# A hybrid decoder layer on one core: the depth of the key loads, the place of the residual loads, and the order of VectorE's small steps

## The reference

```python
h = rms(x, g_pre); z = h @ w_in                     # w_in: 1024 x 3584
ua, va, ga, qb, kb, vb, gb = split(z)               # 512 columns each
ya = gelu(ua) * (tril(w_s) @ rms_group(gelu(va)) + b_s)
yb = attend(qb, kb, vb)                             # prompt: causal; sample: see below
y  = concat(rms(ya) * silu(ga), rms(yb) * silu(gb)) @ w_out
out = x + rms(y, g_post)
```

## Time and profile before

| | us |
|---|---|
| median of three runs | 464.26 |
| lowest and highest of them | 460.81, 469.82 |
| the profiled execution's own time | 458.46 |
| its span, first to last instruction | 456.7 |
| mean granted TensorE clock in it | 0.952 of full speed |

### The profile page before, as it was taken

The page is one execution under the profiler, slowest core; times in us unless marked ns, Lnnn a source line. Parts: engine busy times, 40 slices in busy tenths (PEclk is TensorE's granted clock), DMA queues, the critical chain, the costliest instruction groups (busy, mean ns, idle before and its releaser), DMA issues.

```text
span 456.7 us, 8866 instructions
## 1 busy us (share of the span) xinstructions
PE 404.6 (89%) x2696; PEld 189.1 (41%) x2696; DVE 278.5 (61%) x756; ACT 125.2 (27%) x282; POOL 243.6 (53%) x347
## 2 busy tenths in 40 slices
PE   4898998999599997999998979999699289979993
PEld 2643443434243453445534434444244144434361
DVE  2445494458244596678767875678675975782242
ACT  2411110000121323664656332642461321001110
POOL 4877226661666236751877456734575467672021
PEclk9899998999899999999999997999799689997998
DMA  7999269984999629993999489937999899642121
GB/s 226 408 380 364 77 204 376 343 232 150 315 361 296 192 76 321 346 257 103 292 338 282 123 278 354 280 90 225 346 358 289 238 365 343 175 98 52 46 93 49
DMA packets 79694, 111.24 MB, mean 244 GB/s; under 512 B 46560, under 2 KB 47584, under 8 KB 79648
## 3 DMA queue, kind: packets, MB, share of 16 engines
q0 software_dynamic: 22576, 71.45, 46.0%
q1 hardware_dynamic: 44864, 21.10, 17.7%
q10 hardware_dynamic: 12208, 18.14, 13.4%
HBM read 106.34 MB, written 4.29 MB: 242 GB/s over the span
## 4 chain that ended last, share of the span: by engine, by line
PE 43%; DMA 19%; issue 11%; DVE 10%; POOL 7%; SPq 6%; DVEq 2%; POOLq 1%; ACT 0%; ACTq 0%
PE PA L1027 24%; DMA K<-in_cache_k,kidx 12%; POOL K L890 6%; PE PA L1133 5%; DVE ksum L1609 4%; PE GB L1150 4%; PE SB L981 3%; SPq L774 3%; DMA V<-in_cache_v 2%; DMA V<-in_page_table 2%; PE SB L1081 2%; PE DC L1179 1%; DMA q_rows<-qs 1%; DVEq L1607 1%; PE PO L1103 1%
## 5 line engine op out<-in xcount | busy, mean ns | idle before, releaser
L890 POOL DMA_INDIRECT K<-in_cache_k,kidx x128 | 134.5, 1051 | 128.0 <-DVE ksum L1609 67.8
L1027 PE MATMUL PA<-wbuf,hT 128*128 128x512 f32 x384 | 188.5, 624 | 1.8 <-DMA wbuf<-in_w_in 0.9
L741 DVE TENSOR_TENSOR ksum<-K 128x512 f32<-128x512 f32 x128 | 85.9, 687 | 59.5 <-DMA K<-in_cache_k,kidx 33.8
L1027 PEld LDWEIGHTS PA<-wbuf,hT 128*128 128x128 f32 x384 | 69.1, 196 | 79.6 <-issue 74.9
L726 POOL DMA_DIRECT2D V<-in_cache_v x128 | 76.0, 593 | 32.6 <-issue 24.6
L1133 PE MATMUL PA<-wbuf,hT 128*128 128x512 f32 x128 | 62.1, 627 | 3.1 <-DVE v L1539 2.2
L1609 DVE TENSOR_TENSOR ksum<-K,qb 128x128 f32<-128x128 f32 x192 | 41.9, 286 | 12.6 <-DVE selT L1579 4.8
L1133 PEld LDWEIGHTS PA<-wbuf,hT 128*128 128x128 f32 x128 | 23.9, 199 | 30.4 <-issue 29.9
L1150 PE MATMUL GB<-ksum,win 128*32 128x512 f32 x256 | 34.1, 605 | 1.3 <-DVE ksum L741 1.3
L1027 PE MATMUL PA<-hT,wbuf 128*128 128x512 f32 x64 | 31.0, 630 | 0.0
L1624 DVE TENSOR_REDUCE sc<-ksum 128x48 f32<-128x3072 f32 x8 | 26.8, 3353 | 0.3
(11 more groups left out here) (200 smaller groups left out, 371.1 us busy)
## 6 DMA issues: line engine op xcount, KB each, us to landing
wbuf<-in_w_in ACTq DMA_DIRECT2D x20, 512.0 KB
V<-in_cache_v SPq DMA_DIRECT2D x240, 32.0 KB
V<-in_cache_v POOLq DMA_DIRECT2D x128, 32.0 KB, 3.0
wbuf<-in_w_out ACTq DMA_DIRECT2D x8, 512.0 KB
wbuf<-in_w_in SPq DMA_DIRECT2D x8, 256.0 KB, 8.6
K<-in_cache_k,kidx POOLq DMA_INDIRECT x128, 7.7
wbuf<-in_w_in SPq DMA_DIRECT2D x4, 512.0 KB
qb<-q_rows SPq DMA_DIRECT2D x8, 256.0 KB
```

The source lines that it names most:

```text
L741: eng.tensor_tensor(ksum[:, n % SUMS, :], K[:, n, 0, :], K[:, n, 1, :], ALU.add).then_inc(s_dsum, 1)
L890: pool.indirect_dma_start(K[:, n, :, :].rearrange("p r w -> p (r w)"), None, k_rows, bass.IndirectOffsetOnAxis(ap=kidx[:, b, n:n + 1], axis=0)
L1027: last = pe.matmul(bank[:, :], lhs, rhs, start=(kc == 0), stop=(kc == KC - 1))
```

## The change

The number of key blocks on their way is four. The order of lanes on VectorE is "score norm scale out gate attention groups sample tail". The four pairs of small loads, gpostq and xq, are issued by SyncE among the first loads, after the last of the small weights. The step res becomes five steps, g_post first and then the four residual tiles; they follow the squares of yb in the plan, where before they needed only the last values of the attention. VectorE waits for g_post before the first op, for the residual tiles before the first opf, and for the small loads before the sample's last step. vn has four slots, and the gb chunk uses all four: its tiles 2 and 3 wait for nothing, its tiles 0 and 1 for the ga products of tiles 2 and 3.

```diff
-                if t >= 2 or name == "gb":
-                    deps.append(("DVE", ("pj", c, t - 2) if t >= 2 else ("pj", c - 1, t + 2)))
+                if (name == "ga") == (t >= 2):
+                    deps.append(("DVE", ("pj", 5, t - 2 if name == "ga" else t + 2)))
...
-        add("DVE", "out", ("op", t, half), 0.8, ("ACT", ("op", t, half)), ("ACT", ("res",)))
+        add("DVE", "out", ("op", t, half), 0.8, ("ACT", ("op", t, half)), ("ACT", ("res", 0)))
...
-            add("DVE", "scale", ("opf", t), 1.3, ("POOL", ("op", t, 1)))
+            add("DVE", "scale", ("opf", t), 1.3, ("POOL", ("op", t, 1)), ("ACT", ("res", NT)))
...
-    add("ACT", "fetch", ("res",), 2.5, ("PE", ("pv", H - 2, NT - 1)), ("SP", ("vrow", NT)))
+    for r in range(NT + 1):
+        add("ACT", "fetch", ("res", r), 0.55, ("ACT", ("sq", 1, NT - 1)), ("SP", ("vrow", NT)))
...
-FLIGHT, WP, EARLY_SUMS, ROOT_HOLD, LANDS, LAST_MARGIN = 5, 4, 1.5, 3.0, 1.5, 0.3
+FLIGHT, WP, EARLY_SUMS, ROOT_HOLD, LANDS, LAST_MARGIN = 4, 4, 1.5, 3.0, 1.5, 0.3
...
-DVE_LANES = "score gate attention norm groups out scale sample tail"
+DVE_LANES = "score norm scale out gate attention groups sample tail"
...
-        vn = sb("vn", [P, 2, W])
+        vn = sb("vn", [P, NT, W])
...
+            sp.wait_ge(s_clear, 2)
+            for j in range(4):
+                sp.dma_start(gpostq[32 * j:32 * j + 32, :, :],
+                             gpost_halves[:, :, j, :].broadcast_to([32, 2, P])).then_inc(s_xq, 16)
+                sp.dma_start(xq[32 * j:32 * j + B, :, :], xs_halves[:, :, j, :]).then_inc(s_xq, 16)
...
-                    for t in range(NT):
-                        act.dma_start(xres[t], x_rows[t].rearrange("p (a b) -> p a b", a=2)).then_inc(s_xres, 16)
-                    act.dma_start(gpost, g_post.broadcast_to([P, D])).then_inc(s_xres, 16)
...
+                    r = s[1]
+                    if r == 0:
+                        act.wait_ge(s_ptused, H * NT // 2)
+                        act.wait_ge(s_vrow_stored, 16 * ROWSETS)
+                        act.dma_start(gpost, g_post.broadcast_to([P, D])).then_inc(s_gpost, 16)
+                    else:
+                        act.dma_start(xres[r - 1], x_rows[r - 1].rearrange("p (a b) -> p a b", a=2)).then_inc(s_xres, 16)
...
-                    if name in ("ga", "gb") and (name, t) not in (("ga", 0), ("ga", 1)):
-
-                        act.wait_ge(s_ydone, (c - 5) * NT + t - 1)
+                    if name == "ga" and t >= 2:
+                        act.wait_ge(s_ydone, t - 1)
+                    if name == "gb" and t < 2:
+                        act.wait_ge(s_ydone, NT - 1 + t)
```

More of the change, by code:

```diff
@@ L607, in hymba_kernel @@
         s_xres = sem("x_residual_loaded")
+        s_gpost = sem("g_post_loaded")
+        s_xq = sem("sample_residual_loaded")
         s_yo = sem("y_tile_ready")
@@ L624, in hymba_kernel @@
         xres = [qT[:, 0:2, :], qT[:, 2:4, :], kT[:, 0:2, :], kT[:, 2:4, :]]
-        stage = [pr[:, :, :], pT[:, :, :, :].rearrange("p a j q -> p a (j q)"), v[:, 2:4, :], vn[:, :, :]]
+        stage = [pr[:, :, :], pT[:, :, :, :].rearrange("p a j q -> p a (j q)"), v[:, 2:4, :], vn[:, 0:2, :]]
         gpost = v[:, 0:2, :].rearrange("p a b -> p (a b)")
@@ L1254, in _ @@
                 if kind == "res":
-                    act.wait_ge(s_ptused, H * NT // 2)
-                    act.wait_ge(s_vrow_stored, 16 * ROWSETS)
-                    for t in range(NT):
-                        act.dma_start(xres[t], x_rows[t].rearrange("p (a b) -> p a b", a=2)).then_inc(s_xres, 16)
-                    act.dma_start(gpost, g_post.broadcast_to([P, D])).then_inc(s_xres, 16)
-                    for j in range(4):
-                        act.dma_start(gpostq[32 * j:32 * j + 32, :, :],
-                                      gpost_halves[:, :, j, :].broadcast_to([32, 2, P])).then_inc(s_xres, 16)
-                        act.dma_start(xq[32 * j:32 * j + B, :, :], xs_halves[:, :, j, :]).then_inc(s_xres, 16)
+                    r = s[1]
[5 more added lines that the diff above has]
+                        act.dma_start(xres[r - 1], x_rows[r - 1].rearrange("p (a b) -> p a b", a=2)).then_inc(s_xres, 16)
                 if kind == "xn":
@@ L1293, in _ @@
                                     "ga": (vn[:, t % 2, :], ACT.Silu, rstd[:, t:t + 1]),
-                                    "gb": (vn[:, t % 2, :], ACT.Silu, rstd[:, t:t + 1])}[name]
+                                    "gb": (vn[:, t, :], ACT.Silu, rstd[:, t:t + 1])}[name]
                     act.activation(dst, bank, fn, scale=sc_).then_inc(pa_free[n % 2], 1)
@@ L1464, in _ @@
                         dve.scalar_tensor_tensor(out=y[:, t, :], in0=y[:, t, :], scalar=rstd[:, col:col + 1],
-                                                 in1=vn[:, t % 2, :], op0=ALU.mult, op1=ALU.mult).then_inc(s_ydone, 1)
+                                                 in1=vn[:, t % 2 if name == "ga" else t, :], op0=ALU.mult,
+                                                 op1=ALU.mult).then_inc(s_ydone, 1)
                 elif kind == "spj":
@@ L1534, in _ @@
                     if t == 0 and half == 0:
-                        dve.wait_ge(s_xres, 16 * (NT + 9))
+                        dve.wait_ge(s_gpost, 16)
                     if half == 1:
@@ L1543, in _ @@
                     rstd_wait(("op", t, 1))
+                    if t == 0:
+                        dve.wait_ge(s_xres, 16 * NT)
                     pa_evac_wait(dve, ("op", t, 1))
@@ L1685, in _ @@
                 elif kind == "fop":
-                    dve.wait_ge(s_xres, 16 * (NT + 9))
+                    dve.wait_ge(s_xq, 16 * 8)
                     rstd_wait(("tot", "y"))
```

## The result

The changed kernel took 471.44 us (470.49 to 473.02, 4 runs) against 467.04 us (460.81 to 472.76, 4 runs) for the kernel before: 1.020 of it, 95% interval 1.012 to 1.028. On a second occasion it was 473.00 us against 470.18, ratio 1.008 (1.005 to 1.012). So it is slower, by one to two per cent by these ratios.

The account below looks back on a forecast made before the run. Bound: a never-slack loop of eight batches (key stream, block sums, selection, products). Terms 2.4 + 1.0 + 0.7 − 2.7 − 1.0 + 2.0 − 3.0 = −0.6 us from 464.3 gave 463.7, the same time; range 450 to 476.

Parts of the forecast that it names:

- Four key blocks out: GpSimd's key stream: landing shrinks with the line, 1.62 us per block against 1.66 now, so just enough; +1 us.
- rival B: Key stream: four blocks don't cover landing, a slot turns over in more than 6.6 us; slower, 477 us; chance 0.17.
- the upper bound: Key stream: if landing stays at its least of 7.2 us, 1.95 per block, +35 us in all.
- The range's +10: Key stream: a quarter of the +35 us bound for four blocks out, kept for the range.
- Small loads on SyncE: Eight loads before the q rows on SyncE delay VectorE's first gate from 52.66 to 55.0: +2.4 us, bounds 0 and +4.8.
- dgm gaps: TensorE's idle before the dgm matmul is covered by other work: −2.7 us in batch 5, −1.0 in batch 0.
- The last seam: Start of output projection: later first matmul nets +0.5 us, residual loads in the last key stream +1.5; together +2.0.
- The unnamed pauses: TensorE idle of 4.53, 3.03 and 1.18 us near bursts of five loads gets shorter with four: −3 us, bounds 0 and −15.
- Rival A: TensorE's pauses hang on the burst of five loads, and four end them: faster, 451.7 us; chance 0.27.
- Rival D: The order does nothing on the chip, since engines wait for DMA and not as planned: 464.3 us; 0.42 with the forecast.

Follow-up runs that it names:

- e3: The changed kernel with only 16 of the 512 columns of each half of the residual tiles loaded: 470.49 us, 1.023 of the kernel before.
- e17: The changed kernel itself, run once more on one chip beside the best version: 473.00 us, 1.008 of the kernel before.

## Why the prediction was wrong, step by step

**Four key blocks out: the step that failed, and rival B is what happened.** The prediction let the turn shrink with the depth: it took 5.9 + 0.6 = 6.5 us, from the first block of a batch, so 6.5/4 = 1.62 per block, and a price of +1. That block was issued into an empty line, and the turn of the others didn't shrink: its median over all streams is 8.3 us in the kernel before and 8.1 to 8.4 in the six kernels with four out (8.4 in the changed kernel). A turn of 8.2 over four is 2.05; the measured distance is 1.94 to 2.01, since the first four issues of a batch wait for no landing. "If landing shrinks with the line" seemed to hold (7.7 to 6.3), but these landings are those of the last blocks of a batch. With the median of 7.7 instead of the least, the formula of the upper bound gives (7.7 + 0.6)/4 = 2.08; with 7.2 its 1.95 lay just below what came. The term was +1.0; the issues took +43.1, of which +15.1 reached the last reduction and +12.2 the end of the span. Four out alone costs 1.6 to 1.8 per cent in two runs. Why the turn is no shorter with four, at a lower rate of DMA, stays open.

**The range's +10 and the cover.** What hid two thirds of +43.1 are the shorter time after the last issue (−20.7) and the gate's waits for TensorE (−8.7). The prediction named neither. It gave B 477 and 0.17; measured 471.4, inside the range of 450 to 476, with the wrong sign of the difference.

**Small loads on SyncE: +2.4 forecast, −0.6 measured, for a reason outside the term.** The eight loads took 5.0 us of SyncE (forecast 4.8), and the landing of the last q_rows store was seen 4.4 after its issue (forecast 4.3). But SyncE reached the first of the small weights at 28.48 instead of 34.87, since the loads ahead of them had taken less: gain's issue 1.38 us instead of 4.88. In the other three executions with four out and the loads early it was 32.2 to 33.0, and the gate came 0.1 earlier to 0.6 later than before. With five out and the loads early SyncE was 1.4 to 4.8 us later there than before, the store went out at 49.3 to 52.3 and landed in 1.3, and the gate came at 54.3 to 57.1. So with five the gate came near the forecast 55 or behind it, by a later store and a quicker landing than it took. What makes the difference is the other part of the change: in the seven profiles with four out SyncE reached the small weights at 28.5 to 33.9, in the seven with five out at 34.9 to 39.7. The prediction had no term for that.

**dgm gaps, −2.7 and −1.0: right.** In batch 5 from 3.47 to 0.79, that is −2.7; in batch 0 from 2.25 to 1.27 us, which now stands before the matmul on mx, that is −1.0.

**The last seam, +2.0: right in kind, too small.** The forecast first projection matmul was 12 us after the reduction began; it was 14.5. The term that was off is the landing of block 0 beside the residual loads, 8.5 us for 5.9. e3 puts the loads' share of the last stream at 4.9 us (41.7 to 36.8), the upper end of the term's 0 to 5, though its total doesn't show it.

**The unnamed pauses, −3: the sum right by luck, the mechanism half right.** Both went from the changed kernel's profile (−7.6), one of 4.47 came: −3.1. But in its second profile (e17) that one is 6.37, and with the order of before and four out the first stayed at 3.86. The Trainium skill's rule in "DMA: Bandwidth & Descriptors", section "Queues, rings and completion order", that the engines go round between the queues, made this term 0. The series 0, 0, 3.03, 9.74 us at one instruction, and 1.17 to 5.60 at the other, with three, four, five and six key blocks out speak against 0; that these pauses are waits for another queue's packets is not shown. Rival A was right that they depend on depth, and wrong that four ends them and is the way to profit: the stream pays more.

**Rival D, that the order does nothing, fell.** Lanes in the old order cost three per cent, and the change without its depth gains two (0.981 twice).

## What to carry to other kernels

For a window of transfers, read the turn from issue to issue of the blocks that wait for each other, in the steady part of the stream, and don't take it for granted that it shrinks with the depth: neither the first block nor a landing that the trace has only for the last ones tells. Then try the depth on both sides: here three and six out cost seven per cent each. When a change has several parts, the gain of one can be hidden by the loss of another: here the rest was worth two per cent, and this showed only when the depth was taken back in the plan as well as at run time.

## What the runs showed of the hardware that was not expected

With more gathers of 512 KB out, TensorE's results come late in places where nothing that it needs is named, and VectorE and ScalarE stop with it, while GpSimd and the DMA queues go on: for 3 to 10 us with five and six out, and still for 4 to 6 us with four. With five out the times of a kernel scatter over 9 to 28 us, with four out over 3 to 8, and with three or six over 6 (4 to 23 executions each). The turn of a gather hardly depends on whether four or five are out (8.2 and 8.3 us), and falls only at three (6.7), though DMA's busy share is as full with four as with five. One SyncE load of 256 KB took from 0.5 to 4.9 us to issue, and SyncE was 1 to 11 us sooner through its first loads with four gathers out than with five. Why TensorE is late stays open: no kernel here took the value copies or the queue of SyncE away from it.
